# One core, a two-block model: the order of VectorE's work in the opening stage and ahead of the first state products, and TensorE's fillers beside it

## What is computed

```
mod = silu(c) @ ada_w[0] + ada_b[0]              # shift, scale, gate
h = rms_norm(x, norm_g[0]) * (1 + scale) + shift
z = h @ even_w_in                                 # a_val, a_glu, a_gate, r, k, v, wd, ad, b_gate
ya = conformer_conv(a_val, a_glu, ...) * silu(a_gate)   # 31 taps, causal
yb = rwkv7_mix(r, k, v, wd, ad, ...) * silu(b_gate)     # recurrence over the tokens, 16 heads
x = x + gate * (concat(ya, yb) @ even_w_out)
```

## Time and profile before

| what | value |
|---|---|
| median of three runs | 2021.74 us |
| the profiled execution | 2019.01 us, span 2017.0 us |
| PE busy | 1947.0 us (97%) |
| DVE busy | 1429.3 us (71%) |
| ACT busy | 997.6 us (49%) |
| HBM traffic | 223 GB/s over the span |
| mean granted TensorE clock | 0.992 |

### The profile page before, as it was taken

The page is one execution under the profiler, slowest core; times in us unless marked ns, Lnnn a source line. Parts: engine busy times, 40 slices in busy tenths (PEclk is TensorE's granted clock), DMA queues, the critical chain, the costliest instruction groups (busy, mean ns, idle before and its releaser), DMA issues. The chain is left out here.

```text
span 2017.0 us, 30114 instructions
## 1 busy us (share of the span) xinstructions
PE 1947.0 (97%) x12675; PEld 1771.6 (88%) x12675; DVE 1429.3 (71%) x1724; ACT 997.6 (49%) x1145; POOL 81.1 (4%) x128
## 2 busy tenths in 40 slices
PE   6999989999999999999999999999999999999988
PEld 5888878888888968999999898989898989898976
DVE  6788995564765346665455588888888888888862
ACT  2511111325465212434345476676777767767654
POOL 3010000000000100100220000000000000000000
PEclk9999999999999999999999999999999999999989
DMA  9846221452432422456653389999999999999970
GB/s 339 271 147 200 73 64 43 167 189 105 171 119 87 158 99 81 148 187 191 203 212 109 119 303 350 355 339 349 355 352 342 348 353 356 337 348 356 356 268 21
DMA packets 225858, 452.31 MB, mean 224 GB/s; under 512 B 6944, under 2 KB 91176, under 8 KB 225720
## 3 DMA queue, kind: packets, MB, share of 16 engines
q1 hardware_dynamic: 222400, 445.44, 63.0%
q0 software_dynamic: 1632, 4.75, 0.9%
q10 hardware_dynamic: 1688, 0.15, 0.1%
HBM read 448.21 MB, written 2.10 MB: 223 GB/s over the span
## 5 line engine op out<-in xcount | busy, mean ns | idle before, releaser
L2047 DVE TENSOR_TENSOR ring_r<-ring,his_r 128x2816 fp32r<-128x2816 f32 (+1 forms) x192 | 586.5, 3085 | 39.1 <-ACT his_r L1583 38.9
L1583 ACT ACTIVATE his_r<-ring 128x2816 fp32r<-128x2816 f32 (+1 forms) x192 | 491.3, 2561 | 186.7 <-DMA ring<-in_moe_w_dram 180.4
L1188 PE MATMUL bank<-his_r,hg_r 128*128 128x352 f32 x2048 | 353.4, 324 | 0.0
L1188 PEld LDWEIGHTS bank<-his_r,hg_r 128*128 128x128 f32 x2048 | 332.0, 188 | 0.6
L2544 PE MATMUL bank<-hT,ring 128*128 128x256 f32 x912 | 207.1, 383 | 1.0 <-DVE arena L3129 0.5
L2544 PEld LDWEIGHTS bank<-hT,ring 128*128 128x128 f32 x912 | 169.9, 190 | 27.5 <-issue 4.8
L1188 PE MATMUL bank<-ring_r,hg_r 128*128 128x352 f32 x1024 | 186.2, 324 | 0.0
L1188 PEld LDWEIGHTS bank<-ring_r,hg_r 128*128 128x128 f32 x1024 | 169.2, 189 | 0.0
L3150 DVE SCALAR_TENSOR_TENSOR arena<-ring,cw,arena 128x256 f32<-128x256 f32 x240 | 96.5, 478 | 0.1
L1214 PE MATMUL bank<-his_r,at_hi_r 128*128 128x512 f32 x352 | 93.0, 397 | 0.0
L1214 PE MATMUL bank<-his_r,at_lo_r 128*128 128x512 f32 x352 | 92.5, 396 | 0.0
(11 more groups left out here) (553 smaller groups left out, 2987.4 us busy)
## 6 DMA issues: line engine op xcount, KB each, us to landing
ring<-in_moe_w_dram SPq DMA_DIRECT2D x128, 1408.0 KB, 8.2
ring<-in_moe_w_dram SPq DMA_DIRECT2D x48, 1536.0 KB, 9.0
ring<-in_even_w_in_dram SPq DMA_DIRECT2D x28, 1024.0 KB, 6.5
ring<-in_ffn_w_dram SPq DMA_DIRECT2D x22, 1024.0 KB, 5.3
ring<-in_ada_w_dram SPq DMA_DIRECT2D x20, 1024.0 KB, 10.2
ring<-in_odd_w_in_dram SPq DMA_DIRECT2D x9, 2048.0 KB, 7.7
ring<-in_moe_w_dram SPq DMA_DIRECT2D x16, 1024.0 KB, 7.1
ring<-in_a_w_in_dram SPq DMA_DIRECT2D x6, 2048.0 KB, 8.0
```

What stands on the lines that cost most here:

```text
L1188: ins = mm(bank[first + m][:, 0:WC], x[:, KT // 2 * late + k, :], w[:, k, WC * m:WC * m + WC], start=(not late and k == 0 and s == "hg_hi" ...
L1583: A(moe_hi(n), moe_w(n), ACT.Copy).then_inc(sem("moe_hi"), 1)
L2047: V.tensor_tensor(moe_lo(n), moe_w(n), moe_hi(n).bitcast(F32), ALU.subtract).then_inc(sem("moe_lo"), 1)
```

## The change

On TensorE the turning of the parameters becomes a function and runs after `ada(0)` in place of ahead of it. The filler behind the norm sums goes from 22 to 14 calls, the filler ahead of `lt_pair` from 24 to 8. On VectorE `ada(3, 1)` runs ahead of the reciprocal, and the three AUX sums run behind hT. `ada(8, 0)` moves ahead of XG, `receptance(2)` behind it. Eight instructions of the convolution move from ahead of the second half's br masks to behind them. No instruction of VectorE, ScalarE or SyncE is added or removed.

```diff
+            def turn_params():
+                pe.wait_ge(sem("params_loaded"), 16 * NPAR)
+                pe.wait_ge(sem("pool_params_loaded"), 32)
...
             ada(0)
+            turn_params()
             ada(1)
             for q in range(KT):
                 norm_tile(0, q)
-            keep_busy(6, 22)
+            keep_busy(6, 14)
...
-            keep_busy(3, 24)
+            keep_busy(3, 8)
             pe.wait_ge(sem("rwkv_set"), 1)
...
             ada(3, 0)
+            ada(3, 1)
             dve.wait_ge(sem("norm_rooted"), 1)
             dve.wait_ge(sem("params_taken"), 1)
-            ch(V.tensor_scalar(AUX[:, 0:24], ...))
-            ch(V.tensor_scalar(AUX[:, 24:32], ...))
-            V.tensor_scalar(AUX[:, 32:33], ...).then_inc(sem("aux_ready"), 1)
             step(V.reciprocal(nr[:, :], nr[:, :]))
-            ada(3, 1)
...
             for ct in range(KT):
                 V.scalar_tensor_tensor(hT[:, ct, :], xT[:, ct, :], ...).then_inc(sem("h_scaled"), 1)
+            ch(V.tensor_scalar(AUX[:, 0:24], ...))
+            ch(V.tensor_scalar(AUX[:, 24:32], ...))
+            V.tensor_scalar(AUX[:, 32:33], ...).then_inc(sem("aux_ready"), 1)
...
             receptance(1)
-            receptance(2)
+            ada(8, 0)
             dve.wait_ge(sem("lora_taken"), 16)
             dve.wait_ge(sem("decays"), 2)
             V.tensor_tensor(XG[:, :, :], X2[:, :, :], X3[:, :, :], ALU.mult).then_inc(sem("grown"), 1)
+            receptance(2)
             dve.wait_ge(sem("spread_ready"), 1)
...
-            ada(8, 0)
             receptance(3)
...
-            conv(12)
+            conv(4)
             br_masks(1, 0, 2)
             conv(8)
             br_masks(1, 2, 4)
-            conv(30)
+            conv(38)
             states(1, lambda n, m: FILL1[2 * n + m])
```

More of the change, by code:

```diff
@@ L2508, in _ @@
                     ins.then_inc(sem("turned_in"), 1)
[L2510 to L2515, removed]
+            def turn_params():
+                pe.wait_ge(sem("params_loaded"), 16 * NPAR)
+                pe.wait_ge(sem("pool_params_loaded"), 32)
+                tr(bank[5][:, 0:P], PROW[:, 0, :], ident[:, :])
+                tr(bank[5][:, P:2 * P], PROW[:, 1, :], ident[:, :])
+                tr(bank[5][:, 256:380], CROW[0:124, 0, :], ident[0:124, 0:124])
+                tr(bank[5][:, 380:504], CROW[0:124, 1, :], ident[0:124, 0:124]).then_inc(sem("turned_in"), 1)
             pe.wait_ge(sem("pool_made"), MADE["ones"])
@@ L3112, in _ @@
             ada(3, 0)
+            ada(3, 1)
             dve.wait_ge(sem("norm_rooted"), 1)
             dve.wait_ge(sem("params_taken"), 1)
-            ch(V.tensor_scalar(AUX[:, 0:24], pc[:, VEC["mu_r"]:VEC["mu_r"] + 24], -1.0, 1.0, ALU.mult, ALU.add))
-            ch(V.tensor_scalar(AUX[:, 24:32], cols8("k_a"), -1.0, 1.0, ALU.mult, ALU.add))
-            V.tensor_scalar(AUX[:, 32:33], mulora, -1.0, 1.0, ALU.mult, ALU.add).then_inc(sem("aux_ready"), 1)
             step(V.reciprocal(nr[:, :], nr[:, :]))
-            ada(3, 1)
             dve.wait_ge(sem("pool_made"), MADE["const"])
@@ L3124, in _ @@
                 V.scalar_tensor_tensor(hT[:, ct, :], xT[:, ct, :], gs[:, ct:ct + 1], nr[:, :], ALU.mult, ALU.mult).then_inc(sem("h_scaled"), 1)
+            ch(V.tensor_scalar(AUX[:, 0:24], pc[:, VEC["mu_r"]:VEC["mu_r"] + 24], -1.0, 1.0, ALU.mult, ALU.add))
+            ch(V.tensor_scalar(AUX[:, 24:32], cols8("k_a"), -1.0, 1.0, ALU.mult, ALU.add))
+            V.tensor_scalar(AUX[:, 32:33], mulora, -1.0, 1.0, ALU.mult, ALU.add).then_inc(sem("aux_ready"), 1)
             def lerp(n, name, q, dst, mu):
```

## The result

The changed kernel takes 2010.28 us (median of four executions, 2009.19 to 2011.41) against 2021.97 for the kernel before, a ratio of 0.994 with a 95% interval of 0.9927 to 0.9952. The profiled execution took 2011.41 us, span 2009.4, so between the two traces the gain is 7.6 us and between the medians 11.7. This gap of 4 us is what had to be explained. Three executions further on that took 2447 us (kernel before), 3256 us (e13) and 8382 us (e12) are in no mean or ratio here.

What follows compares the result with a forecast made beforehand. The prediction took hand-overs between TensorE and VectorE at three places to bound the kernel. Its terms -3.1 - 3.4 - 2.2 = -8.7 us gave 2021.7 - 8.7 = 2013.0 us, range 2010 to 2018.5.

Steps and rivals of the forecast that it cites:

- Part 1: Opening stage up to the first projection: reordered sums and parameter turning bring the modulation earlier, -3.1 us (bounds -1.2 and -3.4).
- The wait of 1.82: Opening: VectorE's 1.82 us wait for TensorE's `ada(0)` goes, giving -1.8 us.
- chunk 5: Opening: data landing at 24.07, wanted by VectorE at 24.2; fits by 0.1, loss of up to 0.3 us allowed.
- the near tie between sums and reciprocal: Opening: TensorE's two sums end at 34.4 to 35.2, close to VectorE's reciprocal; can cost 0.3 us.
- the fourth rival: Opening: shorter filler leaves TensorE's clock low into the projections, +12 us there, total 2029; chance 0.08.
- Part 2: Up to the first state products: `ada(8, 0)` fills VectorE's idle time, `lt_pair` comes earlier, -3.4 us (bounds -2.8 and -3.4).
- The idle time ahead of `lt_pair`: TensorE, its filler cut to 16 instructions, idles 1.1 us ahead of `lt_pair`, for 0.80 before.
- Part 3: Second half's masks: mask earlier by eight convolution taps, state addition earlier, -2.2 us (bounds 0 and -2.4).
- VectorE's wait: Second half's first state addition: VectorE's wait of 2.45 us for TensorE's state product shrinks to 0.2.
- the last line of the sum: Whole kernel: the -8.7 us worked out on one trace is taken off the median, 2021.7 - 8.7 = 2013.0.
- My second rival: Past the edits: the gain comes, part is lost at a clock drop further on, 2015 to 2019; chance 0.08.
- the wait of 2.2 us at `br_pair(1, 2)`: Second half: TensorE's whole wait of 2.23 us for VectorE's mask goes.

Runs made afterwards that it cites:

- e13: Changed kernel with the convolution's eight instructions back ahead of the second half's br masks: 2013.74 us, 0.9968 of the kernel before.
- e12: Changed kernel with more TensorE filler after `ada(2)`, ahead of the gate's modulation wait and ahead of the expert gather: 2008.94 us, 0.9942 of the kernel before.
- e1: Kernel before with only the opening's edits (parameter turning, filler 22 to 14, `ada(3, 1)`, AUX): ratio 0.9975.
- e4: Changed kernel with the opening filler back at 22 calls: 2011.11 us, 0.9941 of the kernel before.
- e7: Changed kernel run again unchanged, beside the kernel before: 2010.61 us, ratio 0.995 (0.9936 to 0.9963).
- e6: Kernel before run again unchanged, for a third trace: 2021.96 us.
- e14: Changed kernel with the opening's edits undone: 2014.08 us, 0.9969 of the kernel before.
- e8: Kernel before with `ada(8, 0)` ahead of XG and `receptance(2)` behind it, filler ahead of `lt_pair` left at 24 calls: 2016.76 us, one execution.
- e16: Kernel before with nine filler calls ahead of `br_pair(1, 2)` and four ahead of the gate's modulation wait, no order changed: ratio 0.9988.
- e10: Changed kernel with both opening fillers taken out: 2016.01 us, one execution.
- e2: Kernel before with only the `ada(8, 0)` and `receptance(2)` moves and the filler ahead of `lt_pair` cut to 8: ratio 0.9981.
- e9: Kernel before with only the parameters turned behind `ada(0)`: 2016.12 us, one execution.
- e11: Kernel before with nine filler calls ahead of `br_pair(1, 2)`, no order changed: ratio 0.9998.
- e3: Kernel before with only the convolution's eight instructions moved behind the second half's br masks: ratio 0.9969.

## Why the prediction was right, and where it was not

**Part 1** was sized right against the trace that it was read from: 3.2 in e1 and 3.4 in e4 and e7 for 3.1 forecast. Against the traces of the old opening whose sums ran faster (e6 and e14, modulation at 36.9) it is 2.0 at the modulation, so part of the 3.1 was itself the price of a low pace. The wait of 1.82 went, chunk 5 took 0.26 us of idle time in the changed kernel's trace and none in its second one (e7), and the near tie between sums and reciprocal cost 0.39 where the clock was low and nothing in e1, e4 and e7. What I got half right is the fourth rival: its mechanism came in the profiled execution itself. TensorE ran out of filler, waited 1.90 us, and the clock fell from 33 to 40, for a loss of 2.2 at `lt_pair` against e7. But the old opening, with its full filler, has such a wait and such a fall in six of nine traces, so it was no new risk; and its price was far too high.

**Part 2**: 3.4 forecast. From the first projection to `lt_pair` it took 68.4 us before and 64.8 in e4 and e7: 3.6. The idle time ahead of `lt_pair` stayed at 0.80 where I had 1.1: the filler took 1.95 for 1.84, and the hand-over came 0.2 earlier than worked out.

**Part 3**: the hand-over gave 2.2 to 2.3, as forecast, and VectorE's wait fell to 0.16 (0.2 forecast).

**The step that failed** is the last line of the sum, "against that median the forecast is 2021.7 - 8.7". It carried the difference of one trace over to the median, as if the low stretches were the same before and after. My second rival allowed for a change in their number only upwards. The prediction had noted that its trace lay 2.7 under the median, and gave no reason for it. In fact the trace I read held none of the low stretches at 37, 194 and 300 us that other executions of the same kernel show, and the change removed what stood ahead of one of them: the wait of 2.2 us at `br_pair(1, 2)` costs itself and, in four of eight traces, another 1.6 us at half clock, 0.8 on average. The trace I read also had the wait ahead of the opening's last sums at 0.40 us, where six of nine with the old opening have 1.65 or more. The mechanism of all three parts was right: of the three traces without a low stretch between 31 and 445 us, e8 has part of the change, and the other two, the first of the kernel before and e12, stand 8.7 us apart at line 687 (444.9 and 436.2), or 9.2 with the 0.5 that e12's additional filler costs in the opening. What was missing is a term for the clock, worth about 2 us. With it the sum is 9.0 to 9.3 of hand-overs against the first trace, and about 2 of clock, for 11.0 between the means (2021.5 of 76 executions and 2010.5 of nine, give or take 1). The second comparison alone (7.5 to 12.9 us) would not have shown that anything was missing.

Filler alone gained 2.4 us in e16, at the edge of its interval, and without any in the opening the granted clock lay at 0.50 for 10 us in e10. The Trainium skill (TensorE: Matmul & The Clock Gate, Part 1: The HAM clock gate) states that sustained activity releases the clock and its lack throttles it; these two runs agree, and the fall in e2 with TensorE busy throughout does not.

**What stays open.** How the 2 us of clock divide among the parts isn't settled. The wait at `br_pair(1, 2)` accounts for some 0.8 by the traces, and e11, which filled it, did not show even that in its median; so its share is likely, and not shown by a time. Part 3 alone (e3) gained 4.0 us at the lower end of its interval, more than its 2.2 and that 0.8 together, while leaving it out (e13) costs 3.3 to 4.6; the runs don't say from where the rest comes. In the opening a low stretch began between 32 and 44 us in seven of ten traces with the old opening (e9, with only its parameters turned, among them) and in two of the seven with the new one and its filler. That the wait ahead of the last sums brings it rests on the count over eighteen traces and on e4 and e12, one trace each, where filler closed that wait and no fall came; e4's median doesn't show it. That TensorE's clock fell at 64 us in e2 with the engine busy throughout has no explanation here.

## What to carry to other kernels

At a hand-over between two engines, a shorter order on the waiting side passes on in full only if the filler ahead of the wait is shortened with it; count the filler as work. A wait of 2 us on TensorE costs itself and, in part of the executions, over half as much again (1.6 us for 2.2, in four of eight traces) in clock behind it, so look for the waits that a reordering opens or closes, and fill what is left. Read more than one trace before you carry a difference over to a median: two executions of one kernel lay 7.4 us apart by the same mark, because of three stretches at half clock. A wait that you mean to remove can itself hang on the clock: the 1.82 us of part 1 were 0.36 in another execution.

## What the runs showed of the hardware that I had not expected

- In the trace of before the granted clock reads 1.00 from 24 to 30 us while each instruction of line 2356 took 0.41 us, against 0.22 for the projections. The clock's own records begin at 30.15 in that trace, and at 19.5 in e6, where the sums ahead of the norm ran at twice the pace (1.85 us for 3.42). Ahead of the first record the pace decides.
- A low stretch can follow a wait of only 2.2 us (0.57 over 292 to 296 in e13), and can also stay away after the same wait (the first trace of before).
- In e10, with no filler in the opening, the low stretch of 10 us ended 4 us after the projections began, at a cost of 2.6 us at `lt_pair`.
- A wait of 1.65 to 3.5 us on TensorE in the opening came with a low stretch in nine of ten traces, one of 0.85 or less in one of eight.
